# The last column half of two output products, run token tile by token tile

## Chip, core and metric

The kernel runs on one core of a Trainium2 chip. The metric is the device time of one execution in microseconds: 1674.59 us, the median of three runs of the kernel before (1671.56 to 1675.25).

## What is computed

One inference step of a 2-layer encoder, for a prompt of 256 tokens and 8 samples of 16 tokens (128 rows); width 1024, all in fp32. Shortened:

```
for l in range(2):
    x = x + mixer(rms_norm(x)) @ w_out[l]          # attention, retention and convolution heads, joined
    q = rms_norm(x) @ wx_q[l]                      # cross attention, 4 heads, 256 memory tokens
    x = x + softmax(q @ k_mem) @ v_mem @ wx_o[l]
    h = rms_norm(x)
    x = x + (dense_swiglu(h) if l == 0 else moe_swiglu(h))   # top 2 of 8 experts in layer 1
y = rms_norm(x)
```

The change lies at two places in each layer: the product with `w_out` and what follows it (norm, product with `wx_q`), and the product with `wx_o` and what follows it (norm, dense network or router).

## The kernel before

**Tiles and slabs.** The 384 tokens are three tiles of 128 (`NT` = 3). A weight of 1024 x 1024 comes in four slabs of 128 x 2048 (1 MB): a left and a right column half of 512, and of each two row halves. SyncE fetches the slabs in one fixed order into a ring of four slots (`R`). For slab s it waits for the reader of slab s-4, which the function `slabs` names: for `w_out` the tile of the product whose end frees the slot, for the query and output weights of cross attention the low part (below) that was made of the slab.

**Split products.** An fp32 slab is split in a high part (a copy by ScalarE, `w_high` L926, in the dense network L803) and a low part (a subtraction by VectorE, `w_low` L930, `mix_low` L967, L808). A product of a tile with half a slab's depth is then three matmuls per 128 rows (L1151 to L1153): one column half of one token tile is 8 x 3 = 24 matmuls of 512 columns. The last halves of `out` (`mix_product`) and of `o` (`split_product`) run slab by slab: tiles 0, 1, 2 with the first slab, then tiles 0, 1, 2 with the second.

**Between products.** Per token tile: VectorE adds the product to the residual `x` (`add_x`, L2196, one instruction per column half), ScalarE squares it with a row sum (`squares`, L1724), GpSimd makes the reciprocal root (L2552, L2554), VectorE scales the row (`norm_row`, L2150), TensorE transposes it in eight pieces (`norm`, L1077), ScalarE takes the high part (`h_high`, L1731) and VectorE the low part (`take`, L2162) into `hT_parts`. All of it is in a program order of its own on each engine, written out by hand; nothing is reordered when it runs. `psum_jobs` lists which PSUM bank each product takes and in which order.

**Names at the two places.** `part(l, m, low)` tells where the split query and output slabs m = 0 to 7 lie (0 to 3 the query weight, 4 to 7 the output weight; m = 6, 7 are the right half of the output weight). Before, some of them shared space with others, so `w_high` waited for the end of a product. SyncE waits at L1007 for the last tile of `o` in layer 0, and only then streams the dense network's slabs (L836). `prime` frees the dense network's slots and signals for their first use.

## Time and profile before

| | us |
|---|---|
| median of 3 runs | 1674.59 |
| profiled execution, device time | 1668.94 |
| its span, first to last instruction | 1667.0 |
| TensorE busy in it | 1542.4 (93%) |
| VectorE busy | 1003.5 (60%) |
| ScalarE busy | 747.3 (45%) |
| GpSimd busy | 184.3 (11%) |

The mean granted clock of TensorE is 0.97 of full speed. The share of busy time is a mean over stages with different limits; what a seam between two products is worth is read from the timelines of that seam.

### The profile page before, as it was taken

Reading aid. Unit: us, or ns where it says so; the run is one execution under the profiler, and the core shown is the slowest. Engines: PE = TensorE matmul, PEld = TensorE weight load, DVE = VectorE, ACT = ScalarE, POOL = GpSimd, SP = SyncE. Lnnn points to the kernel's source line nnn. Section 1 sums busy time; section 2 is a strip of 40 time slices with the busy share of each in tenths; the row PEclk is TensorE's granted clock in tenths of the full one; section 3 lists DMA queues with packets and bytes.
Section 4 is the critical chain, followed back from the end, with each engine's and each line's share of the span. In section 5 each row is a group of like instructions: output and inputs, shape, how many; then the busy total and the mean of one; then the engine's idle time right before and its main releaser. Section 6 shows DMA issues by size and latency. Waiting matters only on the chain.

```text
span 1667.0 us, 21420 instructions
## 1 busy us (share of the span) xinstructions
PE 1542.4 (93%) x7995; PEld 1262.3 (76%) x7995; DVE 1003.5 (60%) x1304; ACT 747.3 (45%) x896; POOL 184.3 (11%) x270
## 2 busy tenths in 40 slices
PE   5999999797999999899999997979999999999996
PEld 4875677666998898688567775768887888788875
DVE  3692653444342434359365434367988898888986
ACT  3423333433332333242243343146676667666763
POOL 2351200000000000314220000100000000000001
PEclk9999999998999999899999999869999999999998
DMA  6735354374333333343645329269999999999993
GB/s 225 250 109 189 130 164 152 146 271 156 111 119 120 130 100 110 127 144 125 195 152 173 134 76 353 102 234 332 316 323 320 332 329 329 325 335 335 317 329 124
DMA packets 176576, 347.72 MB, mean 209 GB/s; under 512 B 7114, under 2 KB 48348, under 8 KB 176240
## 3 DMA queue, kind: packets, MB, share of 16 engines
q1 hardware_dynamic: 162224, 316.17, 55.4%
q0 software_dynamic: 5936, 19.92, 3.5%
q10 hardware_dynamic: 8352, 10.75, 1.8%
q8 instruction: 44, 0.72, 0.2%
q14 instruction: 20, 0.16, 0.0%
HBM read 335.20 MB, written 13.48 MB: 209 GB/s over the span
## 4 chain that ended last, share of the span: by engine, by line
PE 59%; issue 22%; DMA 8%; DVE 6%; ACT 3%; POOL 2%; POOLq 0%; SPq 0%; DVEq 0%; ACTq 0%
PE bank L1151 14%; PE bank L1153 14%; PE bank L1152 14%; PE bank L1113 5%; DMA arena<-h_rows,row_of_slot 4%; PE bank L1077 4%; PE bank L1528 2%; DMA ring<-in_cache_mem_k 1%; POOL counts L2609 1%; DMA out_new_mem_k_prompt<-arena 1%; DVE arena L2325 1%; ACT arena L1719 1%; PE bank L1580 1%; PE bank L1649 1%; DVE arena_parts L808 1%
## 5 line engine op out<-in xcount | busy, mean ns | idle before, releaser
L808 DVE TENSOR_TENSOR arena_parts<-ring,arena_parts 128x2048 fp32r<-128x2048 f32 (+1 forms) x156 | 331.3, 2142 | 176.9 <-ACT arena_parts L803 176.9
L1151 PE MATMUL bank<-arena_parts,features_parts 128*128 128x512 f32 (+2 forms) x1056 | 410.5, 389 | 13.1 <-DVE ring_low_parts L967 7.3
L1153 PE MATMUL bank<-arena_parts 128*128 128x512 f32 (+1 forms) x928 | 363.1, 391 | 0.0
L803 ACT ACTIVATE arena_parts<-ring 128x2048 fp32r<-128x2048 f32 (+1 forms) x156 | 277.4, 1796 | 148.3 <-PE bank L1153 132.9
L1152 PE MATMUL bank<-arena_parts 128*128 128x512 f32 (+1 forms) x704 | 258.9, 368 | 0.0
L1152 PE MATMUL bank<-arena_parts,features_parts 128*128 128x512 f32 (+1 forms) x672 | 257.4, 383 | 0.0
L1151 PEld LDWEIGHTS bank<-arena_parts,features_parts 128*128 128x128 f32 x1056 | 201.3, 191 | 51.9 <-issue 11.1
L1153 PEld LDWEIGHTS bank<-arena_parts 128*128 128x128 f32 x928 | 176.2, 190 | 40.1
L1719 ACT ACTIVATE arena<-bank 128x512 f32<-128x512 f32 (+3 forms) x160 | 85.3, 568 | 228.9 <-PE bank L1153 138.4
L1153 PE MATMUL bank<-arena_parts,features_parts 128*128 128x512 f32 (+1 forms) x480 | 182.0, 379 | 0.0
L1152 PE MATMUL bank<-ring_low_parts,features_parts 128*128 128x512 f32 (+1 forms) x384 | 146.6, 382 | 0.0
L1151 PE MATMUL bank<-arena_parts 128*128 128x512 f32 x352 | 141.9, 403 | 5.0 <-DVE arena_parts L808 5.0
L1152 PEld LDWEIGHTS bank<-arena_parts,features_parts 128*128 128x128 f32 x672 | 127.4, 190 | 23.1
L1152 PEld LDWEIGHTS bank<-arena_parts 128*128 128x128 f32 x704 | 133.3, 189 | 14.5
L1151 PE MATMUL bank<-features_parts,arena_parts 128*128 128x384 f32 x352 | 119.4, 339 | 9.5 <-DVE arena_parts L808 9.5
L1077 PE MATMUL bank<-consts,arena 128*128 128x128 f32 (+1 forms) x576 | 81.7, 291 | 48.5 <-DVE arena L2150 17.1
L808 DVE TENSOR_TENSOR arena_parts<-mem_kv,arena_parts 128x2048 fp32r<-128x2048 f32 (+1 forms) x60 | 120.1, 2017 | 5.2 <-ACT arena_parts L803 5.2
L1153 PE MATMUL bank<-features_parts,arena_parts 128*128 128x384 f32 x352 | 119.5, 339 | 0.0
L1077 PEld LDWEIGHTS bank<-consts,arena 128*128 128x128 f32 (+1 forms) x576 | 69.5, 149 | 65.8 <-issue 38.0
L803 ACT ACTIVATE arena_parts<-mem_kv 128x2048 fp32r<-128x2048 f32 (+1 forms) x60 | 102.0, 1700 | 31.2 <-PE bank L1153 31.2
L1153 PEld LDWEIGHTS bank<-arena_parts,features_parts 128*128 128x128 f32 x480 | 90.6, 189 | 14.7
L967 DVE TENSOR_TENSOR ring_low_parts<-ring,arena_parts 128x2048 fp32r<-128x2048 f32 (+1 forms) x32 | 69.5, 2172 | 45.1 <-ACT arena_parts L962 44.8
(288 smaller groups left out, 1913.0 us busy)
## 6 DMA issues: line engine op xcount, KB each, us to landing
ring<-in_moe_w_up SPq DMA_DIRECT2D x40, 1024.0 KB, 6.2
ring<-in_moe_w_down SPq DMA_DIRECT2D x30, 1024.0 KB, 5.2
ring<-in_w_in SPq DMA_DIRECT2D x20, 1024.0 KB, 7.4
ring<-in_moe_w_gate SPq DMA_DIRECT2D x20, 1024.0 KB, 7.4
mem_kv<-in_moe_w_gate SPq DMA_DIRECT2D x20, 1024.0 KB, 9.1
ring<-in_cache_mem_k SPq DMA_DIRECT2D x16, 1024.0 KB, 7.4
ring<-in_cache_mem_v SPq DMA_DIRECT2D x16, 1024.0 KB, 8.0
ring<-in_moe_w_gate SPq DMA_DIRECT2D x20, 768.0 KB, 5.7
```

The source lines that it names most:

```text
L803: nc.scalar.activation(self.part(s, 0), self.raw(s), ACT.Copy).then_inc(self.high, 1)
L808: nc.vector.tensor_tensor(self.part(s, 1), self.raw(s), self.part(s, 0).bitcast(F32), ALU.subtract).then_inc(self.split["v"], 1)
L967: nc.vector.tensor_tensor(low, raw, high.bitcast(F32), ALU.subtract).then_inc(s_msplit, 1)
L1077: return nc.tensor.transpose(out, src, ident[0:src.shape[0], 0:src.shape[0]])
L1113: ins = nc.tensor.matmul(out[:, 0:w], left(k, t), wt[:, k - k0, :], start=(g == 0 and k == k0), stop=(g == len(groups) - 1 and k == k0 + n ...
L1151: nc.tensor.matmul(out, left[0], right[0], start=start, stop=False)
L1152: nc.tensor.matmul(out, left[0], right[1], start=False, stop=False)
L1153: return nc.tensor.matmul(out, left[1], right[0], start=False, stop=stop)
L1528: ins = nc.tensor.matmul(b[:, :], memT[:, k, t * P:(t + 1) * P], wt[:, k - 4 * g, :], start=(k == 0), stop=(k == KC - 1))
L1580: ins = nc.tensor.matmul(b[:, i * 256:(i + 1) * 256], qxT[:, 2 * h + k, (j // 2) * P:(j // 2 + 1) * P], mkT[:, 2 * h + k, :], start=(k == ...
L1649: ins = nc.tensor.matmul(b[:, i * 256:(i + 1) * 256], mv[:, mt, (2 * h + i) * P:(2 * h + i + 1) * P], pxT[:, h, mt, :], start=(mt == 0), s ...
L1719: st.emptied(A(out, in_, ACT.Copy), *key)
```

## The change

It makes five moves.

- The right halves of `out` and `o` run tile by tile (`last_chunk`): each tile with both slabs, then the next. Tile 0's transposes stand ahead of tile 2's matmuls. With it, the slot of the third slab of `w_out` is freed by the last tile instead of the first (`slabs`).
- The transposes of tiles 1 and 2 ahead of `q` move: tile 1's stand before the first tile of `q`, tile 2's behind it.
- VectorE takes tile 0 and scales tile 1 between the residual adds; at the seam to `q` the low part of the query slab m = 2 now stands ahead of the scaled row of tile 2.
- The slabs m = 6 and 7 get space of their own, so their parts are made before `o`'s right half, and their low parts stand around its first residual add.
- SyncE's wait before the dense slabs is gone; in layer 0 the slots are freed right behind m = 7's low part.

```diff
@@ psum_jobs
+    def tiles_last(name, n):
+        product(name, 1, NT, "v")
+        for t in range(NT):
+            if t == NT - 1:
+                norm(n, (0,))
+            jobs.append((name + (1, t), (3 * (big[0] % 2) + t,), "v"))
+        big[0] += 1
...
@@ slabs
-                last = tiles - 1 if half or (c == 0 and key[0] == "in") else 0
+                last = tiles - 1 if half or (c == 0 and key[0] == "in") or (c == 1 and key[0] == "out") else 0
...
@@ part, w_high
-        OWN_AT = {(4, 0): 2 * NT * D, (4, 1): n_.at, (5, 0): 0, (5, 1): n_.at + SLAB, (7, 0): 2 * NT * D, (7, 1): n_.at}
+        OWN_AT = {(4, 0): 2 * NT * D, (4, 1): n_.at, (5, 0): 0, (5, 1): n_.at + SLAB,
+                  (6, 0): n_.at - 3 * SLAB, (6, 1): n_.at - 2 * SLAB, (7, 0): n_.at - SLAB, (7, 1): n_.at + 2 * SLAB}
...
-            if m >= NSPLIT and m not in (4, 5):
-                q = m - NSPLIT
-                key = ("q", l, 0, NT - 1) if q < 2 else ("q", l, 1, NT - 1 if q == 3 else 0) if q < 4 else ("o", l, 0, NT - 1)
-                wait_filled(act, *key)
+            if m == NSPLIT:
+                wait_filled(act, "q", l, 0, NT - 1)
+            elif m >= 6:
+                wait_filled(act, "xss", l, 3)
...
@@ SyncE
                 if s == at_layer:
-                    wait_filled(sp, "o", 0, 1, NT - 1)
                     with sp.Fori(0, half_ffn.n) as i:
...
@@ TensorE
+            def last_chunk(key, n, left, slabs_):
+                wt = []
+                for t in range(NT):
+                    if t == NT - 1:
+                        norm(n, (0,))
+                    b = begin(*key, 1, t)
+                    for g in range(2):
+                        if t == 0:
+                            wt.append(slabs_[g]())
+                        ins = split_tile(b, left, 4 * g, wt[g], t)
+                    end(ins, *key, 1, t)
...
-                for c in range(2):
-                    mix_product(("out", l), l, MIX + 2 * c, hT_parts, 512, c,
-                                {2: ("obT", l, 1), 4: ("obT", l, 3)} if c == 0 else {})
-
-                norm(3 * l + 1, (0,))
+                mix_product(("out", l), l, MIX, hT_parts, 512, 0, {2: ("obT", l, 1), 4: ("obT", l, 3)})
+                last_chunk(("out", l), 3 * l + 1, hT_parts, [lambda: mix_slab(l, MIX + 2), lambda: mix_slab(l, MIX + 3)])
+
+                norm(3 * l + 1, (1,))
                 wt = [w_parts(l, m) for m in range(2)]
                 for t in range(NT):
+                    if t == 1:
+                        norm(3 * l + 1, (2,))
                     wait_emptied(pe, "hT", 3 * l + 1, t, 1)
                     b = begin("q", l, 0, t)
                     for g in range(2):
-                        if g and t < NT - 1:
-                            norm(3 * l + 1, (t + 1,))
                         ins = split_tile(b, hT_parts, 4 * g, wt[g], t)
...
-                split_product(("o", l), l, 6, oT_parts, 1)
-
+                last_chunk(("o", l), 3 * l + 2, oT_parts, [lambda: w_parts(l, 6), lambda: w_parts(l, 7)])
+
+                wait_emptied(pe, "hT", 3 * l + 2, 0, 1)
                 (routed if l % 2 else half_ffn).prime(turn(bank[7][:, 0:P], ident))
-                norm(3 * l + 2)
+                norm(3 * l + 2, (1, 2))
...
@@ ScalarE, at both seams
-                squares(3 * l + 1, (0, 1))
+                squares(3 * l + 1, (0,))
                 h_high(3 * l + 1, (0,))
-                squares(3 * l + 1, (2,))
+                squares(3 * l + 1, (1, 2))
...
@@ VectorE, norm_T
+                if n % 3:
+                    take(1)
+                    if n % 3 == 1:
+                        w_low(dve, n // 3, 2)
+                    norm_row(n, 2)
+                    take(2)
+                    if n % 3 == 1:
+                        w_low(dve, n // 3, 3)
+                    return
...
@@ VectorE, add_x
                         if (c, t) == (1, 0):
                             norm_row(n, 0)
+                        if (c, t) == (1, 1):
+                            take_T(n, 0)
+                            norm_row(n, 1)
...
-                        if name == "o" and (c, t) in ((0, 0), (0, NT - 1)):
-                            w_low(dve, l, 6 + (t > 0))
+                        if name == "o" and (c, t) == (0, 0):
+                            w_low(dve, l, 7)
+                            if l == 0:
+                                half_ffn.prime(V.memset(full[:, 2:3], 0.0), "split")
...
@@ VectorE, before add_x of "o"
                 values_low(3)
+                w_low(dve, l, 6)
                 add_x("o", l, 3 * l + 2)
```

VectorE from the two low parts of the query slabs m = 0, 1 (L930) to those of m = 2 and 3, before (L2196 is the residual add, L2150 the scaled row, L2162 the low part of a transposed tile):

```order
L930 TENSOR_TENSOR arena_parts<-ring,arena_parts 128x2048 [waits cross_slab_high_part_ready] x2
L2196 TENSOR_TENSOR x<-bank,x 128x512 [waits psum_filled]
L2150 SCALAR_TENSOR_TENSOR arena<-x,stat,arena 128x1024 [waits rstd_ready,gain_row_in1]
L2196 TENSOR_TENSOR x<-bank,x 128x512 [waits psum_filled] x2
L2162 TENSOR_TENSOR arena_parts<-bank,features_parts 128x4x128 [waits h_high_part_ready,psum_filled] x2
L2150 SCALAR_TENSOR_TENSOR arena<-x,stat,arena 128x1024 [waits rstd_ready] x2
L2162 TENSOR_TENSOR arena_parts<-bank,features_parts 128x4x128 [waits h_high_part_ready,psum_filled] x2
L930 TENSOR_TENSOR arena_parts<-ring,arena_parts 128x2048 [waits cross_slab_high_part_ready]
L2162 TENSOR_TENSOR arena_parts<-bank,features_parts 128x4x128 [waits h_high_part_ready,psum_filled] x2
L930 TENSOR_TENSOR arena_parts<-ring,arena_parts 128x2048 [waits cross_slab_high_part_ready]
```

The same stretch of VectorE after (L940, L2225, L2172 and L2183 are the same four):

```order
L940 TENSOR_TENSOR arena_parts<-ring,arena_parts 128x2048 [waits cross_slab_high_part_ready] x2
L2225 TENSOR_TENSOR x<-bank,x 128x512 [waits psum_filled]
L2172 SCALAR_TENSOR_TENSOR arena<-x,stat,arena 128x1024 [waits rstd_ready,gain_row_in1]
L2225 TENSOR_TENSOR x<-bank,x 128x512 [waits psum_filled]
L2183 TENSOR_TENSOR arena_parts<-bank,features_parts 128x4x128 [waits h_high_part_ready,psum_filled] x2
L2172 SCALAR_TENSOR_TENSOR arena<-x,stat,arena 128x1024 [waits rstd_ready]
L2225 TENSOR_TENSOR x<-bank,x 128x512 [waits psum_filled]
L2183 TENSOR_TENSOR arena_parts<-bank,features_parts 128x4x128 [waits h_high_part_ready,psum_filled] x2
L940 TENSOR_TENSOR arena_parts<-ring,arena_parts 128x2048 [waits cross_slab_high_part_ready]
L2172 SCALAR_TENSOR_TENSOR arena<-x,stat,arena 128x1024 [waits rstd_ready]
L2183 TENSOR_TENSOR arena_parts<-bank,features_parts 128x4x128 [waits h_high_part_ready,psum_filled] x2
L940 TENSOR_TENSOR arena_parts<-ring,arena_parts 128x2048 [waits cross_slab_high_part_ready]
```

The transposed tile 0 and the scaled row of tile 1 now stand between the residual adds, and the low part of m = 2 stands ahead of the scaled row of tile 2, not behind it.

TensorE at the end of `out`, before (L1077 is a transpose of tile 0, the matmuls behind it are the first of `q`):

```order
L1152 MATMUL bank<-arena_parts,features_parts 128x512
L1153 MATMUL bank<-arena_parts 128x512
L1077 MATMUL bank<-consts,arena 128x128 [waits psum_emptied_by_vector,h_ready]
L1077 MATMUL bank<-consts,arena 128x128 x3
L1077 MATMUL bank<-consts,arena 128x128 [waits psum_emptied_by_vector]
L1077 MATMUL bank<-consts,arena 128x128 x3
L1151 MATMUL bank<-arena_parts,features_parts 128x512
L1152 MATMUL bank<-arena_parts,features_parts 128x512
L1153 MATMUL bank<-arena_parts 128x512
```

TensorE after, at the end of tile 1 of `out`'s right half (L1086 the transposes of tile 0, L1160 to L1162 behind them tile 2 of `out`):

```order
L1160 MATMUL bank<-arena_parts,features_parts 128x512
L1161 MATMUL bank<-ring_low_parts,features_parts 128x512
L1162 MATMUL bank<-arena_parts 128x512
L1086 MATMUL bank<-consts,arena 128x128 [waits psum_emptied_by_vector,h_ready]
L1086 MATMUL bank<-consts,arena 128x128 x3
L1086 MATMUL bank<-consts,arena 128x128 [waits psum_emptied_by_vector]
L1086 MATMUL bank<-consts,arena 128x128 x3
L1160 MATMUL bank<-arena_parts,features_parts 128x512 [waits psum_emptied_by_vector]
L1161 MATMUL bank<-ring_low_parts,features_parts 128x512
```

The transposes of tile 0 have 24 matmuls of `out` behind them, and the wait for the scaled row (`h_ready`) stands inside the product.

## Rows read from the trace of the kernel before

**Rows 1.** The page: the span, and the chain that ended last, by engine.

```profile
span 1667.0 us, 21420 instructions
...
PE 59%; issue 22%; DMA 8%; DVE 6%; ACT 3%; POOL 2%; POOLq 0%; SPq 0%; DVEq 0%; ACTq 0%
```

**Rows 2.** TensorE timeline, `out` to `q` (last row layer 1): start, us, instruction, idle.

```profile
252.64 0.39 PE L1152 MATMUL bank<-ring_low_parts,features_parts 128*128 128x512 f32 x1
...
254.24 0.39 PE L1153 MATMUL bank<-arena_parts 128*128 128x512 f32 x1
254.47 1.03 PE L1077 MATMUL bank<-consts,arena 128*128 128x128 f32 x8
257.35 0.47 PE L1151 MATMUL bank<-arena_parts,features_parts 128*128 128x512 f32 x1 [1.85 <-DVE arena_parts L2162]
...
932.36 0.47 PE L1151 MATMUL bank<-arena_parts,features_parts 128*128 128x512 f32 x1 [1.85 <-DVE arena_parts L2162]
```

**Rows 3.** Timeline of TensorE, `o` to the dense product, layer 0.

```profile
392.83 1.04 PE L1077 MATMUL bank<-consts,arena 128*128 128x128 f32 x8
...
399.39 1.94 PE L1077 MATMUL bank<-consts,arena 128*128 128x128 f32 x8 [0.92 <-DVE arena_parts L2162]
407.74 0.68 PE L1151 MATMUL bank<-features_parts,arena_parts 128*128 128x384 f32 x1 [6.41 <-DVE arena_parts L808]
```

**Rows 4.** Timeline of VectorE, the same stretch.

```profile
405.31 4.49 DVE L808 TENSOR_TENSOR arena_parts<-ring,arena_parts 128x2048 fp32r<-128x2048 f32 x2 [2.54 <-ACT arena_parts L803]
```

**Rows 5.** Timeline of ScalarE, same stretch.

```profile
393.46 1.09 ACT L1731 ACTIVATE features_parts<-bank 128x512 fp32r<-128x512 f32 x2 [0.16 <-PE bank L1077]
394.44 1.06 ACT L1724 ACTIVATE arena<-x 128x1024 f32<-128x1024 f32 x1
...
402.07 1.28 ACT L803 ACT_TABLE_LOAD   x1
403.37 5.51 ACT L803 ACTIVATE arena_parts<-ring 128x2048 fp32r<-128x2048 f32 x3
```

**Rows 6.** Waits of SyncE's queue, 350 to 420 us: total, times, longest.

```profile
SPq L1007 <- PE bank L1153: 36.8, 1, 36.8
```

**Rows 7.** DMA issues: size, median us to landing: q2; third dense slab.

```profile
ring<-in_wx_q SPq DMA_DIRECT2D x1, 1024.0 KB, 4.9
...
ring<-in_ffn_w_up SPq DMA_DIRECT2D x1, 1024.0 KB, 10.7
```

**Rows 8.** Timeline of VectorE, `out` to `q`, layer 0.

```profile
245.17 2.29 DVE L930 TENSOR_TENSOR arena_parts<-ring,arena_parts 128x2048 fp32r<-128x2048 f32 x1 [1.86 <-ACT arena_parts L926]
249.17 0.69 DVE L2196 TENSOR_TENSOR x<-bank,x 128x512 f32<-128x512 f32 x1 [1.71 <-PE bank L1153]
252.10 1.29 DVE L2150 SCALAR_TENSOR_TENSOR arena<-x,stat,arena 128x1024 f32<-128x1024 f32 x1 [2.24 <-POOL stat L2554]
...
263.78 2.29 DVE L930 TENSOR_TENSOR arena_parts<-ring,arena_parts 128x2048 fp32r<-128x2048 f32 x1 [0.94 <-ACT arena_parts L926]
```

**Rows 9.** Timeline of TensorE, `o` to the router, layer 1.

```profile
1075.58 1.94 PE L1077 MATMUL bank<-consts,arena 128*128 128x128 f32 x8 [0.72 <-DVE features_T L2164]
```

**Rows 10.** Timeline of SyncE: the issue of slab q2, layer 0.

```profile
249.16 0.37 SPq L1038 DMA_DIRECT2D ring<-in_wx_q  x1
```

**Rows 11.** Timeline of ScalarE, layer 0: high part of q2.

```profile
261.83 1.92 ACT L926 ACTIVATE arena_parts<-ring 128x2048 fp32r<-128x2048 f32 x1
```

**Rows 12.** Windows: busy time and count by engine, granted clock, DMA.

```profile
core 0: us, PE busy (x) PEld busy (x) DVE busy (x) ACT busy (x) POOL busy (x), PEclk, DMA share, GB/s
...
257.35:261.00 3.65, 3.65 (x20) 3.06 (x21) 2.22 (x2) 0.14 (x1) 1.52 (x2) 1.00 1.06 419
...
932.36:937.00 4.64, 4.64 (x15) 3.64 (x16) 2.21 (x2) 0.00 (x0) 1.52 (x2) 0.63 1.04 416
...
397.00:407.70 10.70, 3.41 (x16) 2.64 (x14) 6.33 (x8) 8.10 (x9) 0.93 (x2) 0.50 0.77 292
```

**Rows 13.** Timeline of TensorE in the key stage, layer 0.

```profile
334.71 1.54 PE L1077 MATMUL bank<-consts,ring 128*128 128x128 f32 x6 [5.30 <-DMA ring<-in_cache_mem_k]
```

More of the change, by code:

```diff
@@ L228, in psum_jobs @@
             wide(("obT", l, b), "v")
-        product(("out", l), 2, NT, "v")
-        norm(3 * l + 1, range(NT - 1))
+        tiles_last(("out", l), 3 * l + 1)
+        norm(3 * l + 1, (1,))
         first_chunk(("q", l), 3 * l + 1)
@@ L261, in psum_jobs @@
         wide(("xvT", l, 3), "v")
-        product(("o", l), 2, NT, "v")
-        norm(3 * l + 2)
+        tiles_last(("o", l), 3 * l + 2)
+        norm(3 * l + 2, (1, 2))
         if l % 2:
@@ L1545, in _ @@
                 wait_emptied(pe, "ocT", l, 1)
-                for c in range(2):
-                    mix_product(("out", l), l, MIX + 2 * c, hT_parts, 512, c,
-                                {2: ("obT", l, 1), 4: ("obT", l, 3)} if c == 0 else {})
-                norm(3 * l + 1, (0,))
+                mix_product(("out", l), l, MIX, hT_parts, 512, 0, {2: ("obT", l, 1), 4: ("obT", l, 3)})
+                last_chunk(("out", l), 3 * l + 1, hT_parts, [lambda: mix_slab(l, MIX + 2), lambda: mix_slab(l, MIX + 3)])
+                norm(3 * l + 1, (1,))
                 wt = [w_parts(l, m) for m in range(2)]
                 for t in range(NT):
+                    if t == 1:
+                        norm(3 * l + 1, (2,))
                     wait_emptied(pe, "hT", 3 * l + 1, t, 1)
@@ L1677, in _ @@
                     end(split_tile(bank[BANK[("o", l, 0, t)][0]], oT_parts, 4, wo[1], t), "o", l, 0, t)
-                split_product(("o", l), l, 6, oT_parts, 1)
+                last_chunk(("o", l), 3 * l + 2, oT_parts, [lambda: w_parts(l, 6), lambda: w_parts(l, 7)])
+                wait_emptied(pe, "hT", 3 * l + 2, 0, 1)
                 (routed if l % 2 else half_ffn).prime(turn(bank[7][:, 0:P], ident))
-                norm(3 * l + 2)
+                norm(3 * l + 2, (1, 2))
                 wait_emptied(pe, "hT", 3 * l + 2, NT - 1, 1)
@@ L2013, in _ @@
                 w_high(act, l, 7)
-                squares(3 * l + 2, (0, 1))
+                squares(3 * l + 2, (0,))
                 if l % 2 == 0:
                     h_high(3 * l + 2, (0,))
-                squares(3 * l + 2, (2,))
+                squares(3 * l + 2, (1, 2))
                 act.wait_ge(s_st, 16 * 8 * (l + 1))
@@ L2151, in norm_row, with take_T, norm_T @@
                                               ALU.mult, ALU.mult), s_h)
-            def norm_T(n, rows_left=NT):
-                def take(t):
-                    for half in range(2):
-                        wait_filled(dve, "hT", n, t, half)
-                        at_ = (slice(None), slice(4 * half, 4 * half + 4), slice(t * P, (t + 1) * P))
-                        b = bank[BANK[("hT", n, t, half)][0]][:, :].rearrange("p (k n) -> p k n", k=4)
-                        if n < 5:
-                            dve.wait_ge(s_hpart, 2 * NT * n + 2 * t + half + 1)
-                            ins = V.tensor_tensor(hT_parts[1][at_], b, hT_parts[0][at_].bitcast(F32), ALU.subtract)
-                        else:
-                            ins = V.tensor_copy(hT[at_], b)
-                        st.emptied(ins, "hT", n, t, half)
+            def take_T(n, t):
+                for half in range(2):
+                    wait_filled(dve, "hT", n, t, half)
+                    at_ = (slice(None), slice(4 * half, 4 * half + 4), slice(t * P, (t + 1) * P))
+                    b = bank[BANK[("hT", n, t, half)][0]][:, :].rearrange("p (k n) -> p k n", k=4)
+                    if n < 5:
+                        dve.wait_ge(s_hpart, 2 * NT * n + 2 * t + half + 1)
+                        ins = V.tensor_tensor(hT_parts[1][at_], b, hT_parts[0][at_].bitcast(F32), ALU.subtract)
+                    else:
+                        ins = V.tensor_copy(hT[at_], b)
+                    st.emptied(ins, "hT", n, t, half)
+            def norm_T(n):
+                def take(t):
+                    take_T(n, t)
+                if n % 3:
[7 more added lines that the diff above has]
+                    return
                 if n == 3:
                     mix_low(dve, 1, 0)
-                if rows_left == NT:
-                    norm_row(n, 0)
+                norm_row(n, 0)
                 if n == 3:
@@ L2180, in norm_T @@
                 take(1)
-                if n in (1, 4):
-                    w_low(dve, n // 3, 2)
                 take(2)
-                if n in (1, 4):
-                    w_low(dve, n // 3, 3)
-                if n in (0, 3):
-                    mix_low(dve, n // 3, 2)
+                mix_low(dve, n // 3, 2)
             def add_x(name, l, n):
@@ L2457, in _ @@
                 add_x("out", l, 3 * l + 1)
-                norm_T(3 * l + 1, NT - 1)
+                norm_T(3 * l + 1)
                 wait_filled(dve, "q", l, 1, NT - 1)
@@ L2529, in _ @@
                 values_low(3)
+                w_low(dve, l, 6)
                 add_x("o", l, 3 * l + 2)
-                (routed if l % 2 else half_ffn).prime(V.memset(full[:, 2:3], 0.0), "split")
-                norm_T(3 * l + 2, NT - 1)
+                if l % 2:
+                    routed.prime(V.memset(full[:, 2:3], 0.0), "split")
+                norm_T(3 * l + 2)
                 if l % 2:
```

## Prediction

> **What bounds the kernel now.** I read the page first: TensorE leads the chain that ended last, with 59%, in a span of 1667.0 us [rows 1]. Where TensorE runs without a gap only fewer matmuls would help, and the change keeps them all. So the question is where TensorE waits. I therefore read the four seams that the change touches, in TensorE's timeline, and then the engines that end its waits. (q0 to q3 are the four half slabs of the query weight, o6 and o7 the last two of the output weight; a "turn" is a transpose by TensorE, eight per token tile and 1.03 us for the eight.)
>
> At the seam from `out` to `q`, matmuls follow each other every (254.24 - 252.64) / 7 = 0.229 us, then comes tile 0's turn, and then a wait of 1.85 us that VectorE ends; it is 1.85 in layer 1 too [rows 2]. That is all there is to gain at this seam: 1.85 us a layer, plus what the clock loses after it. At the seam behind `o` in layer 0, TensorE is free at 392.83 and the dense product begins at 407.74, its last wait 6.41 us long and ended by VectorE's low part of a weight slab [rows 3]. VectorE in turn had waited 2.54 us for ScalarE [rows 4], which did the turned rows' high parts, then a table load of 1.28 us at 402.07, and the first slab's high part at 403.37 [rows 5].
>
> **The early dense stream.** SyncE waited 36.8 us for the end of `o` before it issued the first dense slab [rows 6], and now issues it once the low part of o7 is done, behind the first residual add of `o`: some 20 us earlier (three tiles of 5.5 us and the rest of the left half). I price this at nothing. ScalarE reaches the first slab only after all turned rows and the table load, and before that load it isn't waiting for a transfer [rows 5]; the order of its work there stays, but for one Square that goes behind tile 0's high part. Even the third slab of the burst took only 10.7 us [rows 7], so it had landed some 2 us after ScalarE took the first, and before its turn. What a faster first slab could give would be the idle time of ScalarE, which is not there. The transfers now run beside `o`, where TensorE reads weights that have already landed, so I see no price either.
>
> **The `o` seams.** With tiles run one by one, tile 0's turn (1.03) sits ahead of tile 2's matmuls and needs nothing new: its row is ready long before. Tile 2 then ends at 392.83 + 1.03 = 393.86 instead of 392.83, since the turn itself has only changed places. From there the chain to tile 2's own turn is: about 0.1 to start the residual add, 0.69 for it (as in [rows 8]), 1.06 for ScalarE's Square and some 0.2 to read its sum, 1.09 for tile 1's high part, which now comes behind that Square [rows 5], 0.6 for the last piece of tile 1's low part, and 1.29 for the normed row. That is 393.86 + 4.95 = 398.8, against 399.39 [rows 3]. So -0.6 us; the rest of the seam follows unchanged. In layer 1 the same turn begins at 1075.58 [rows 9] and I take -0.6 again, although no high part stands in that chain. Together **-1.2**, between 0 (the row later by half a microsecond) and -3 (turns at full clock).
>
> **The `q` seams.** Here the change moves three things, and each runs into a queue. I work them out for layer 0.
> - Left half of `out` filled: slab q2 went out at 249.16, when tile 0's right half was done [rows 10], 48 matmuls after the left half, so that was at 249.16 - 48 x 0.229 = 238.2. The tiles of the right half are now filled at 238.2 + 24 x 0.229 = 243.7 and at 249.2.
> - VectorE's residual add of tile 0 stands behind the low part of q1, which ends at 245.17 + 2.29 = 247.46 [rows 8]. Before, that cost nothing, since the tile came at 249.17. From that add to the normed row went 252.10 + 1.29 - 249.17 = 4.22 us [rows 8]. So the row is there at 247.46 + 4.22 = 251.7, while TensorE is free for its turn at about 249.0: **a new wait of 2.7 us**. Turn and tile 2 then run to 251.7 + 1.03 + 5.5 = 258.2.
> - Slab q2's ring slot was released by the first tile of `out`'s right half; since all three tiles now read both halves, the reader is the last tile. It is issued at about 258.4 instead of 249.16, lands 4.9 us later [rows 7], at 263.3, and takes 1.92 on ScalarE [rows 11] and 2.29 on VectorE [rows 8]: 267.5. On VectorE the normed row of tile 2 is queued behind that low part. It ends at 267.5 + 1.29 = 268.8. TensorE meanwhile does tile 1's turn and the first tile of `q`: 258.2 + 1.03 + 5.5 = 264.8. Next on TensorE is tile 2's turn: **a new wait of 4.0 to 4.1 us**. The wait of 1.85 is gone.
>
> So 2.7 + 4.1 - 1.85 = +5.0 a layer. Layer 1 has the same rows 675.0 us later, so **+10.0**. Bounds: 4 to 6 a layer, that is 8 to 12, by a landing that is up to half a microsecond either way and the pieces between instructions.
>
> **The clock.** After the same wait of 1.85 the window of layer 0 shows a granted clock of 1.00, that of layer 1 0.63 [rows 12]: the lower level, 1.2 GHz, for a part of it, which cost 4.64 x (1 - 0.63) = 1.7 us. After the gaps behind `o` the clock was 0.50 [rows 12]. There will be four new waits, all longer than 1.85. The two of 4.1 I count as followed by such a stretch, of the two of 2.7 one: 3 x 1.7 - 1.7 = **+3.4**, between -1.7 (none) and +5.1 (all four). The Trainium skill, page "TensorE: Matmul & The Clock Gate", section "What's actually happening", says that the throttled state is the default and that activity releases it. By that alone every one of the four would pay, and this term would be +5.1, the sum 13.9; layer 0's window at 1.00 after a wait shows that not every wait does.
>
> **Sum.** 10.0 + 3.4 - 1.2 = 12.2 us. The profiled execution took 1668.94 us (a span of 1667.0 and 1.94 around it), 5.65 below the median of 1674.59, so its 12.2 would give 1681.1 there; I add them to the median, and round: **1687**. From the bounds, 8 - 1.7 - 3 = +3 and 12 + 5.1 + 0 = +17: 1678 to 1692.
>
> **Rivals.** (1) Faster: the seams close as they are laid out. If q2 were split by the time tile 0 of `q` ends, and q1's low part did not hold the add, TensorE would have neither wait: 2 x -1.85 - 1.7 - 1.2 = -6.6, so 1668. The point is q2's landing: its two splits and the row take 1.92 + 2.29 + 1.29 = 5.5, so it must have landed by 264.8 - 5.5 = 259.3, 0.9 us after its issue. For it speaks that everything else on that path is short; against it, the 4.9 [rows 7]. It holds also if the slot is released earlier than I read. 0.09.
> (2) No change: the delay is absorbed by a later wait that doesn't move. In the key stage TensorE waits 5.30 us for a transfer [rows 13]; two such would take the 10 us back, and leave 1674.6 + 3.4 - 1.2 = 1677 or less. Against it: the slot of that transfer is released by TensorE's own reads, so it moves along. 0.08.
> (3) Slower still: q2, q3 and the first two key slabs are now issued in one burst and share the bandwidth. If q2 lands like the third of a burst, 10.7 instead of 4.9 [rows 7], TensorE waits 5.8 longer in each layer: 1687 + 11.6 = 1698.6. Against it: in the one burst there is, the later slabs took the longer time. The Trainium skill, page "DMA: Bandwidth & Descriptors", section "Queues, rings and completion order", says that each DMA engine consumes descriptors in ring order, which by itself would put q2 first; no run here has shown that for this burst. 0.05.
>
> **How the numbers follow.** The forecast gets 0.78. A difference below 0.2% (3.3 us) can't be told from none; the forecast's low end just touches that, for 0.01. Faster 0.09 from rival 1; same 0.08 + 0.01 = 0.09; slower 0.77 + 0.05 = 0.82. The range goes from 1675 (half of rival 2 with it) to 1692, and leaves out rival 1, rival 3 and half of rival 2, some 0.18.
>
> **What would show it.** In the trace after: a wait of TensorE of about 2.7 us before the turn ahead of tile 2 of `out`, ended by a normed row, and one of about 4 us one tile into `q`, ended by the normed row of tile 2, which starts as the low part of q2 ends; ScalarE waiting for the transfer of q2, issued at the end of `out`; a granted clock well below 1 in `q`. Behind `o`, dense slabs issued at some 373 instead of 393.8 and the dense product beginning only 0.6 us earlier relative to the end of `o`. I am wrong if q2 is issued inside `out`, if the normed row of tile 2 precedes q2's low part, or if the dense product starts several microseconds sooner.

## The result: 1683.71 us after, 1671.56 before

Five runs each: 1683.71 us (1681.42 to 1687.70) against 1671.56 (1668.81 to 1675.25). The ratio is 1.0073, with a 95% interval of 1.005 to 1.0097: 12.15 us slower, between 8 and 16. The forecast was +12.2; the time that went with it, 1687, lies 3.3 us higher since it started from 1674.59, the median of three runs. One of out_only's six runs (below) fell into a slower state (2231.77 us at a mean granted clock of 0.65), so its time is the median of the other five. Of the two executions with a profile, that of before (1668.94) lies as low as the lowest of these five (1668.81) and that of after is the longest of its own (1687.70), so their 18.8 us are not the difference of the kernels; a second profile of before, below, shows what of it is chance.

### The seam from `out` to `q`, after

TensorE's timeline of after, layer 0 and then layer 1 (start, duration, instruction, idle time before it and what ended it). It answers to [rows 2], where one wait of 1.85 us stood in each layer:

```profile
254.39 1.97 PE L1086 MATMUL bank<-consts,arena 128*128 128x128 f32 x8 [2.53 <-DVE arena L2172]
...
262.43 1.03 PE L1086 MATMUL bank<-consts,arena 128*128 128x128 f32 x8
...
273.10 1.97 PE L1086 MATMUL bank<-consts,arena 128*128 128x128 f32 x8 [4.04 <-DVE arena L2172]
...
941.35 1.09 PE L1086 MATMUL bank<-consts,arena 128*128 128x128 f32 x8 [2.50 <-DVE arena L2172]
...
958.52 1.97 PE L1086 MATMUL bank<-consts,arena 128*128 128x128 f32 x8 [4.10 <-DVE arena L2172]
```

At 254.39 stands the turn of tile 0, ahead of tile 2 of `out`; at 262.43 tile 1's, with no wait; at 273.10 tile 2's, one tile into `q`. Waits of 2.53 and 4.04 us, and 2.50 and 4.10 in layer 1: all four are ended by VectorE's scaled row (L2172).

VectorE's timeline of the same stretch, layer 0 (L940 is a low part, L2225 the residual add, L2172 the scaled row), which answers to [rows 8]:

```profile
247.91 2.29 DVE L940 TENSOR_TENSOR arena_parts<-ring,arena_parts 128x2048 fp32r<-128x2048 f32 x1 [1.88 <-ACT arena_parts L936]
250.12 0.68 DVE L2225 TENSOR_TENSOR x<-bank,x 128x512 f32<-128x512 f32 x1
253.05 1.28 DVE L2172 SCALAR_TENSOR_TENSOR arena<-x,stat,arena 128x1024 f32<-128x1024 f32 x1 [2.24 <-POOL stat L2590]
...
269.56 2.29 DVE L940 TENSOR_TENSOR arena_parts<-ring,arena_parts 128x2048 fp32r<-128x2048 f32 x1 [3.17 <-ACT arena_parts L936]
271.77 1.28 DVE L2172 SCALAR_TENSOR_TENSOR arena<-x,stat,arena 128x1024 f32<-128x1024 f32 x1
```

The add of tile 0's right half begins at 250.12, as the low part of q1 ends, with no idle time before it; the row follows, 250.12 to 254.33 = 4.2 us. At 271.77 the scaled row of tile 2 begins as the low part of q2 ends. Why that was late shows in the timelines of SyncE and ScalarE and in the DMA issues (size, us to landing), which answer to [rows 10], [rows 11] and [rows 7]:

```profile
262.63 0.37 SPq L1047 DMA_DIRECT2D ring<-in_wx_q  x1
```

```profile
267.61 1.91 ACT L936 ACTIVATE arena_parts<-ring 128x2048 fp32r<-128x2048 f32 x1 [2.13 <-DMA ring<-in_wx_q]
```

```profile
ring<-in_wx_q SPq DMA_DIRECT2D x1, 1024.0 KB, 5.0
```

q2 is issued at 262.63, when the last tile of `out` is done, lands 5.0 us later, and ScalarE, idle for 2.13 us until then, makes the high part to 269.52.

Windows behind the four waits of after (busy time and count by engine, granted clock, DMA share, GB/s), and behind the two waits of before, which answer to [rows 12]:

```profile
core 0: us, PE busy (x) PEld busy (x) DVE busy (x) ACT busy (x) POOL busy (x), PEclk, DMA share, GB/s
254.39:262.40 8.01, 8.01 (x32) 6.80 (x33) 3.21 (x4) 2.23 (x4) 0.75 (x2) 0.79 0.01 2
...
273.10:285.00 11.90, 11.90 (x45) 9.86 (x46) 1.38 (x2) 2.38 (x4) 0.00 (x0) 0.78 0.37 146
941.35:949.30 7.95, 7.95 (x43) 6.80 (x44) 3.81 (x5) 2.71 (x5) 0.75 (x2) 1.00 0.06 4
...
958.52:970.00 11.48, 11.48 (x42) 9.52 (x43) 1.38 (x2) 2.37 (x4) 0.00 (x0) 0.75 0.39 152
```

```profile
257.35:269.00 11.65, 11.65 (x59) 9.64 (x60) 6.77 (x7) 4.58 (x6) 1.52 (x2) 1.00 0.78 288
...
932.36:944.00 11.64, 11.64 (x51) 9.50 (x52) 5.79 (x5) 3.62 (x5) 1.52 (x2) 0.85 0.66 247
```

What such a window, full of matmuls, loses to the clock is its length times one less the granted clock. After: 8.01 x 0.21 = 1.7, 11.9 x 0.22 = 2.6, nothing, and 11.48 x 0.25 = 2.9, together 7.2 us. Before: nothing, and 11.64 x 0.15 = 1.75.

### The seam behind `o`, after

TensorE in layer 0, which answers to [rows 3]; the turn of tile 1, the turn of tile 2, the first matmul of the dense product:

```profile
406.84 1.04 PE L1086 MATMUL bank<-consts,arena 128*128 128x128 f32 x8
411.93 1.97 PE L1086 MATMUL bank<-consts,arena 128*128 128x128 f32 x8 [4.05 <-DVE arena L2172]
420.30 0.68 PE L1160 MATMUL bank<-features_parts,arena_parts 128*128 128x384 f32 x1 [6.41 <-DVE arena_parts L817]
```

ScalarE in the same stretch ([rows 5]) and the issue of the dense slabs by SyncE:

```profile
413.94 0.60 ACT L1753 ACTIVATE features_parts<-bank 128x512 fp32r<-128x512 f32 x1 [0.26 <-PE bank L1086]
...
414.64 1.28 ACT L812 ACT_TABLE_LOAD   x1
415.94 5.51 ACT L812 ACTIVATE arena_parts<-ring 128x2048 fp32r<-128x2048 f32 x3
```

```profile
385.76 1.03 SPq L845 DMA_DIRECT2D ring<-in_ffn_w_gate  x2
```

From the first of these turns to the dense product it was 407.74 - 392.83 = 14.91 us before and is 420.30 - 406.84 = 13.46 now, of which 1.03 are the turn of tile 0 that was only moved ahead. The dense slabs are issued at 385.76, 21 us ahead of the end of `o` instead of 1 us behind it, and the last wait is 6.41 us as before: ScalarE comes from its last high part almost straight (one small instruction between) to the table load and the first slab.

### The profile page after: what moved, and what is told of

Same layout as the page of the kernel before. It is cut to its first block, busy times and chain, and to the rows that moved or that the text cites. A ratio compares the mean times of both kernels' runs of the same rounds, so it can differ in the third digit from the quotient of the medians.

```text
span 1685.8 us, 21422 instructions
## 1 busy us (share of the span) xinstructions
PE 1547.6 (92%) x7995; PEld 1266.7 (75%) x7995; DVE 1004.0 (60%) x1304; ACT 747.4 (44%) x896; POOL 183.4 (11%) x270
## 4 chain that ended last, share of the span: by engine, by line
PE 57%; issue 22%; DMA 10%; DVE 6%; ACT 3%; POOL 2%; POOLq 0%; SPq 0%; DVEq 0%; ACTq 0%
PE bank L1160 13%; PE bank L1161 13%; PE bank L1162 13%; PE bank L1122 5%; DMA arena<-h_rows,row_of_slot 4%; PE bank L1086 4%; DMA ring<-in_cache_mem_k 2%; PE bank L1550 2%; DMA ring<-in_wx_q 1%; POOL counts L2645 1%; DMA ring<-in_cache_mem_v 1%; DMA out_new_mem_k_prompt<-arena 1%; DVE arena L2359 1%; PE bank L1601 1%; PE bank L1670 1%
## 5 line engine op out<-in xcount | busy, mean ns | idle before, releaser
L1160 PE MATMUL bank<-arena_parts,features_parts 128*128 128x512 f32 (+2 forms) x1056 | 411.8, 390 | 12.1 <-DVE ring_low_parts L977 10.0
L1162 PE MATMUL bank<-arena_parts 128*128 128x512 f32 (+1 forms) x928 | 363.3, 391 | 0.0
L1160 PEld LDWEIGHTS bank<-arena_parts,features_parts 128*128 128x128 f32 x1056 | 202.1, 191 | 50.5 <-issue 7.0
L1162 PEld LDWEIGHTS bank<-arena_parts 128*128 128x128 f32 x928 | 176.9, 191 | 40.2
L1162 PE MATMUL bank<-arena_parts,features_parts 128*128 128x512 f32 (+1 forms) x480 | 181.6, 378 | 0.0
L1160 PE MATMUL bank<-arena_parts 128*128 128x512 f32 x352 | 141.9, 403 | 5.0 <-DVE arena_parts L817 5.0
L1086 PE MATMUL bank<-consts,arena 128*128 128x128 f32 (+1 forms) x576 | 81.3, 290 | 61.9 <-DVE arena L2172 32.2
L1160 PE MATMUL bank<-features_parts,arena_parts 128*128 128x384 f32 x352 | 120.9, 343 | 9.5 <-DVE arena_parts L817 9.5
L1086 PEld LDWEIGHTS bank<-consts,arena 128*128 128x128 f32 (+1 forms) x576 | 68.7, 148 | 79.5 <-issue 37.2
L1162 PE MATMUL bank<-features_parts,arena_parts 128*128 128x384 f32 x352 | 120.1, 341 | 0.0
L1162 PEld LDWEIGHTS bank<-arena_parts,features_parts 128*128 128x128 f32 x480 | 90.5, 189 | 14.9
```

The costliest lines, as they stand in the source:

```text
L1086: return nc.tensor.transpose(out, src, ident[0:src.shape[0], 0:src.shape[0]])
L1160: nc.tensor.matmul(out, left[0], right[0], start=start, stop=False)
L1162: return nc.tensor.matmul(out, left[1], right[0], start=False, stop=stop)
```

## Two executions of the kernel before

**before_again.** The kernel before, unchanged.

> The kernel before, unchanged, for a second profile of it: how far do two executions differ stage by stage? Its first profiled execution (1668.94) lies low among its 23 timed runs (median 1672.8). Theory (the stretches at the lower clock differ from execution to execution, behind the same waits): the waits of the seams repeat within 0.1 us, and the stages that differ by over 1 us are those with another granted clock, the start of the dense product among them. Rival: the waits themselves differ.

It took 1673.98 us. The table gives the time between landmarks in TensorE's timeline, each the first instruction behind a wait that every trace shows; an entry is the difference of two starts.

| stretch | before | before_again | after | row0_first |
|---|---|---|---|---|
| start to the sample's keys | 158.98 | 160.66 | 160.46 | 159.28 |
| to the cross attention, through `out` and `q` | 138.80 | 138.80 | 148.96 | 136.74 |
| to the sample's memory keys | 36.93 | 36.98 | 36.95 | 36.99 |
| to the dense product, through `o` | 73.03 | 73.22 | 73.93 | 74.61 |
| to its second pass | 142.35 | 145.32 | 144.36 | 142.60 |
| to layer 1 | 144.66 | 144.66 | 145.80 | 144.67 |
| to the sample's keys, layer 1 | 137.74 | 137.40 | 136.85 | 136.22 |
| through `out` and `q`, layer 1 | 141.84 | 141.87 | 147.83 | 138.19 |
| to the memory keys | 37.02 | 36.90 | 37.07 | 36.88 |
| through `o` to the expert numbers | 81.99 | 82.30 | 80.42 | 81.47 |
| to the end | 573.66 | 573.89 | 573.17 | 573.45 |

Between the two executions of one kernel the start differs by 1.7 us, the first dense pass by 3.0, all else by at most 0.35. The waits at the four seams repeat, as the theory said (1.85 and 6.41 us in both). One far ahead of them doesn't: in the products ahead of `out` TensorE waits 2.41 us in one and 4.60 in the other for VectorE's low parts, and goes on at 116.00 and at 117.14; that is 1.1 of the start's 1.7. So of the 18.8 us between the profiles 1.5 (start) and 2.0 (first dense pass) are of the kind that one kernel shows by itself; the 1.1 of the second pass these two executions don't show (144.66 in both), the last section does. The change is in the rows through `out` and `q`: +10.2 and +6.0.

Of the +10.2, 1.2 us lie at the start of that stretch, where the kernel is the same, from the sample's keys to the next wait that all traces show (windows of after, then before; the granted clock is third from the end):

```profile
160.46:169.44 8.98, 7.80 (x76) 5.14 (x76) 6.71 (x14) 4.00 (x8) 0.00 (x0) 0.81 0.38 119
...
158.98:166.72 7.74, 6.30 (x77) 4.24 (x77) 6.68 (x14) 3.89 (x8) 0.00 (x0) 1.00 0.43 135
```

This piece takes 7.74 us in nine of the fourteen traces and 8.94 to 8.98 in five, both_moved and row0_first_o_before among them, so it goes with neither the waits at `q` nor the order at `o`. What is left, 8.9 + 6.0 = 14.9 us, is what the four waits and the windows behind them add up to: 2.53 + 4.04 + 2.50 + 4.10 - 2 x 1.85 = 9.5 of waits and 7.2 - 1.75 = 5.4 of clock.

## One part alone

**out_only**: only `out` and its seam to `q` are new. (This cut and the others show the lines that matter of an edit; against the changed kernel where nothing else is said.)

```diff
-        tiles_last(("o", l), 3 * l + 2)
-        norm(3 * l + 2, (1, 2))
+        product(("o", l), 2, NT, "v")
+        norm(3 * l + 2)
...
-                last_chunk(("o", l), 3 * l + 2, oT_parts, [lambda: w_parts(l, 6), lambda: w_parts(l, 7)])
+                split_product(("o", l), l, 6, oT_parts, 1)
```

> The changed kernel with everything at `o` and behind it as before: only `out` and its seam to `q` are new. Theory (the loss lies in VectorE's queue at the seam to `q`, twice): the kernel before plus 2 x 5.0 of waits and about 3.4 of clock, 1671.6 + 13.4 = 1685, with TensorE's waits of 2.5 and 4.0 us in both layers as in the changed kernel. Rival (the early dense stream and the new order at `o` share in the loss): half of it, about 1678 to 1679.

1687.87 us against 1672.81, ratio 1.0089 (1.0072 to 1.0106): +15, between 12 and 18; in the stretches through `out` and `q` +9.95 and +5.8 (with the 1.2 at the start, as in after). The loss lies there whole.

**o_only**: only `o`, its slabs' space and the early dense stream are new.

```diff
-        tiles_last(("out", l), 3 * l + 1)
-        norm(3 * l + 1, (1,))
+        product(("out", l), 2, NT, "v")
+        norm(3 * l + 1, range(NT - 1))
...
-                last = tiles - 1 if half or (c == 0 and key[0] == "in") or (c == 1 and key[0] == "out") else 0
+                last = tiles - 1 if half or (c == 0 and key[0] == "in") else 0
```

> The changed kernel with `out` and its seam to `q` as before: only `o`, the space of the slabs 6 and 7, and the early dense stream are new. Theory: -1.2 us, 1670.4, between 1668 and 1672; the dense product begins some 0.5 us sooner against the end of `o`, the first dense slab is issued 20 us sooner. Rival (early transfers collide, or the dense product starts at the lower clock for longer, as it did in the trace after by 2 us): +2 to +4, 1674 to 1676.

1667.35 us, ratio 0.997 (0.9956 to 0.9985): -5.5, between -2.5 and -7.4, more than the forecast's -1.2.

**o_only_sp_wait**: the early stream undone in it (the line against o_only).

```diff
                 if s == at_layer:
+                    wait_filled(sp, "o", 0, 1, NT - 1)
```

> o_only with SyncE's wait for the end of `o` put back ahead of the dense slabs: the early dense stream alone is undone. o_only was 5.5 us below the kernel before, where -1.2 had been forecast. Theory (the early stream brings nothing, ScalarE reaches the first slab no sooner): the same as o_only, 1667 to 1668. Rival (the early stream is the part that gains): back to -1.5, about 1671.

1668.47 us, ratio 0.9977 (0.996 to 0.9993). The 1.1 us between the two medians can't be told from nothing, and the interval, 1666.3 to 1671.8, just holds the rival's 1671 as well. What speaks for the theory is the trace: the wait ahead of the dense product is 6.41 us here, in o_only and in the kernel before alike, wherever the slabs are issued.

**o_only_again** repeats o_only.

> o_only once more, for what the part at `o` is worth: by the seams in the traces, 1.0 to 2.5 us less than the kernel before, 1669 to 1670.5; by the medians of o_only and o_only_sp_wait 4.5 to 5.5 less, 1666 to 1667. In its trace the cadence of the matmuls in the dense product, at a granted clock of 1.00, is either 0.173 or 0.177 us, as in the two executions of the kernel before (0.1733 and 0.1767); if the new order sets the faster one, it is 0.173 again.

1669.58 us, ratio 0.9983 (0.9967 to 1.0), the cadence (last section) 0.1756: neither of the two. So the new order doesn't set it.

## The two waits, one by one

**row2_first**: on VectorE the scaled row of tile 2 stands ahead of the low part of q2.

```diff
                     take(1)
-                    if n % 3 == 1:
-                        w_low(dve, n // 3, 2)
                     norm_row(n, 2)
+                    if n % 3 == 1:
+                        w_low(dve, n // 3, 2)
                     take(2)
```

> The changed kernel with one edit on VectorE: at the seam to `q` the scaled row of tile 2 stands ahead of the low part of q2. Theory: the wait of 4.0 us ahead of tile 2's turn goes in both layers, the clock loss behind it too: 1683.7 - 8.1 - 3.4 = 1672. Rival (the late landing of q2 is the bound itself, or tile by tile order costs TensorE time by itself): TensorE waits for q2 a few microseconds later instead, 1682 to 1684.

1670.56 us, ratio 0.9987 (0.9972 to 1.0002): 13 us less than after, for one swap; the two waits (4.04 + 4.10) and the clock behind them (2.6 + 2.9) come to 13.6. TensorE's turns of tiles 0 and 2, layer 0, and VectorE's scaled row of tile 2 and low part of q2:

```profile
253.00 1.09 PE L1086 MATMUL bank<-consts,arena 128*128 128x128 f32 x8 [2.39 <-DVE arena L2172]
...
265.90 1.03 PE L1086 MATMUL bank<-consts,arena 128*128 128x128 f32 x8
```

```profile
263.29 1.27 DVE L2172 SCALAR_TENSOR_TENSOR arena<-x,stat,arena 128x1024 f32<-128x1024 f32 x1
266.61 2.29 DVE L940 TENSOR_TENSOR arena_parts<-ring,arena_parts 128x2048 fp32r<-128x2048 f32 x1 [2.04 <-ACT arena_parts L936]
```

The wait of 4 us is gone, that of 2.4 stays. q2 is split as late as before (266.61 to 268.90), and nobody waits for it: its late landing held TensorE only through the row that stood behind it.

**q1_behind_add**: the other wait alone.

```diff
                             w_low(dve, l, 0)
-                            w_low(dve, l, 1)
...
                         if (c, t) == (1, 0):
+                            if name == "out":
+                                w_low(dve, l, 1)
                             norm_row(n, 0)
```

> The changed kernel with the low part of q1 behind the residual add of tile 0's right half; the scaled row of tile 2 stays behind the low part of q2. Theory: the wait ahead of tile 0's turn falls from 2.5 to 0.7 us in both layers, the one of 4.0 us behind it stays at about 4 and keeps its clock loss: both_moved plus 2 x 4.0 and 2 to 6 us of clock, 1674 to 1678. Rival (the two waits are not independent: tile 2 ends sooner, so q2 is issued sooner and the second wait shrinks as well): 1668 to 1670.

1678.13 us, ratio 1.0039 (1.0022 to 1.0055). The turns of tiles 0 and 2 in layer 0:

```profile
252.26 0.98 PE L1086 MATMUL bank<-consts,arena 128*128 128x128 f32 x7 [0.50 <-DVE arena L2172]
...
269.44 1.43 PE L1086 MATMUL bank<-consts,arena 128*128 128x128 f32 x8 [4.10 <-DVE arena L2172]
```

The first wait falls to 0.50 and the second stays at 4.10 (0.57 and 4.21 in layer 1): the two are independent.

**both_moved**: both edits.

> As row2_first, and the low part of q1 stands behind the residual add of tile 0's right half instead of ahead of it. Theory: the wait of 2.5 us ahead of tile 0's turn goes too, in both layers, with its clock loss: no wait over 0.5 us is left at the seam to `q`, where the kernel before has 1.85 twice and 1.7 of clock in one layer: 1671.6 - 3.7 - 1.7 - 1.2 = 1665. Rival (something next in line, such as the low part of q1 for the second half of tile 0 of `q`, or the key stage's transfers, takes it back): 1671 to 1673.

1663.5 us, ratio 0.9953 (0.9938 to 0.9968): 9 us faster than the kernel before, where 1665 was expected. 0.74 us of wait are left ahead of tile 0's turn in layer 0.

**row0_first**: both_moved, with the low part of q1 behind the scaled row of tile 0 too (the cut against both_moved).

```diff
                         if (c, t) == (1, 0):
-                            if name == "out":
-                                w_low(dve, l, 1)
                             norm_row(n, 0)
+                            if name == "out":
+                                w_low(dve, l, 1)
```

> both_moved with one more swap on VectorE: the scaled row of tile 0 stands ahead of the low part of q1, not behind it. Theory: the last wait at the seam, 0.74 us ahead of tile 0's turn, goes in both layers: 1663.5 - 1.5 = 1662. Rival (the low part of q1 is then late for the first tile of `q`, or the residual add of tile 1 behind it): 1664 to 1667.

1662.5 us, ratio 0.9941 (0.9918 to 0.9965). The turns of tiles 0 and 2 in layer 0, and ScalarE's high part of q2:

```profile
249.27 1.04 PE L1086 MATMUL bank<-consts,arena 128*128 128x128 f32 x8
...
262.13 1.03 PE L1086 MATMUL bank<-consts,arena 128*128 128x128 f32 x8
```

```profile
260.85 1.91 ACT L936 ACTIVATE arena_parts<-ring 128x2048 fp32r<-128x2048 f32 x1 [2.15 <-DMA ring<-in_wx_q]
```

No turn waits, and q2's high part begins at 260.85, with its wait for the transfer still there, off TensorE's path. This is the lowest time of those tried, some 21 us below the changed kernel, though its 1 us below both_moved is within the spread of either.

**row0_first_o_before**: the same with `o` as before.

> row0_first with `o` and everything behind it as before: what the part at `o` is worth on another base. By the seams in the traces (1.9 us less from the end of `o` to the next product, over both layers): 1662.5 + 1.9 = 1664.4. By the medians of o_only and o_only_sp_wait: 1662.5 + 5 = 1667.5.

1666.56 us, ratio 0.9971 (0.9956 to 0.9986): the part at `o` is worth 4 us here, between the two expectations and not able to tell them apart, since row0_first's own interval is some 4 us either way.

## The clock apart from the waits

**filled_waits**: the changed kernel with its waits, but TensorE turns the identity matrix while it waits.

```diff
                     if t == NT - 1:
+                        if key[0] == "out":
+                            b = begin(*key, 1, t)
+                            for _ in range(17):
+                                turn(b[:, 0:P], ident)
                         norm(n, (0,))
...
                     if t == 1:
+                        b = begin("q", l, 0, t)
+                        for _ in range(29):
+                            turn(b[:, 0:P], ident)
                         norm(3 * l + 1, (2,))
```

> The changed kernel, all its waits kept, but TensorE turns the identity matrix into the bank of its next product while it waits: 17 times ahead of tile 0's turn at `out`, 29 times one tile into `q` (some 2.2 and 3.7 us), in both layers. What it computes is the same. Theory (the waits cost 9.5 us, and another 7.2 at the lower clock behind three of the four in the trace after): the two long waits end at the same time as before, the clock behind them stays at 1.00, 1683.7 - 5 to 7 = 1677 to 1679. Rival (the clock behind a wait doesn't hang on what TensorE does in it, or the fillers come too late): 1683 or more.

1676.47 us, ratio 1.0032 (1.0018 to 1.0045): 7.2 less than after. TensorE in layer 0, and two windows of the same stretch:

```profile
250.74 2.02 PE L1086 MATMUL bank<-consts 128*128 128x128 f32 x17
253.45 1.09 PE L1086 MATMUL bank<-consts,arena 128*128 128x128 f32 x8 [0.69 <-DVE arena L2179]
...
266.35 3.33 PE L1086 MATMUL bank<-consts 128*128 128x128 f32 x29
270.89 1.09 PE L1086 MATMUL bank<-consts,arena 128*128 128x128 f32 x8 [1.22 <-DVE arena L2179]
```

```profile
251.00:262.00 11.00, 10.31 (x63) 8.80 (x61) 5.15 (x6) 3.38 (x8) 1.50 (x4) 1.00 0.08 8
...
271.00:283.00 12.00, 12.00 (x56) 9.83 (x57) 1.29 (x2) 2.15 (x4) 0.00 (x0) 1.00 0.34 134
```

From free to the turn it is 250.74 to 253.45 = 2.7 and 266.35 to 270.89 = 4.5 us, no shorter than the waits of after (in layer 1 2.6 and 4.2), and the clock is 1.00 behind all four. So the waits keep their price, and what went is the clock's: 7.2 us by the medians, each known to 2 to 4 us, and 7.2 by the windows above.

**row0_first_filled**: row0_first, with the same filling behind `o` in layer 0 (the cut against row0_first).

```diff
-                norm(3 * l + 2, (1, 2))
+                spare = bank[BANK[("o", l, 0, 0)][0]]
+                norm(3 * l + 2, (1,))
+                if l == 0:
+                    for _ in range(29):
+                        turn(spare[:, 0:P], ident)
+                norm(3 * l + 2, (2,))
+                if l == 0:
+                    for _ in range(45):
+                        turn(spare[:, 0:P], ident)
```

> row0_first with the same filling behind `o` in layer 0: 29 turns of the identity between the turns of tiles 1 and 2, 45 behind tile 2's. Theory: the turn of tile 2 runs at full clock (about 0.9 us sooner to the dense product), and the dense product starts at full clock (0.79 to 0.90 over its first 14 us so far, 1.4 to 2.9 us): 1662.5 - 3 = 1659.5. Rival (the fillers reach beyond the waits or the low clock has another cause): 1662 to 1664.

1662.85 us, ratio 0.9947 (0.993 to 0.9964): no gain that can be measured against row0_first. TensorE, and the window of the dense product's start:

```profile
395.24 3.33 PE L1086 MATMUL bank<-consts 128*128 128x128 f32 x29
399.46 1.09 PE L1086 MATMUL bank<-consts,arena 128*128 128x128 f32 x8 [0.88 <-DVE arena L2180]
400.38 5.08 PE L1086 MATMUL bank<-consts 128*128 128x128 f32 x45
407.01 0.44 PE L1160 MATMUL bank<-features_parts,arena_parts 128*128 128x384 f32 x1 [1.55 <-DVE arena_parts L817]
```

```profile
411.00:425.00 14.00, 14.00 (x81) 14.00 (x81) 2.56 (x2) 5.42 (x7) 0.00 (x0) 1.00 0.68 236
```

The clock does stay at 1.00, into the dense product. But that pass took 142.78 us, row0_first's, with a start at the lower clock, 142.60. In this execution the matmuls themselves came slower (last section: 529 of them, 0.0034 us each, 1.8 us), which took back what the start had won; whether several profiles would show the gain is open.

## Why the prediction was right

- **The waits** (+10.0 forecast): +9.5. Each came where it was put, behind the instruction that was named, and row2_first and q1_behind_add remove them one by one.
- **The clock** (+3.4): the count was right, three stretches of four; the size was not. They cost 1.7, 2.6 and 2.9 us rather than 1.7 each, so the term is +5.4, just beyond its upper bound of 5.1. The step that failed was to price a stretch behind a wait of 4 us by one behind a wait of 1.85. What the Trainium skill says in "TensorE: Matmul & The Clock Gate", section "What's actually happening" (throttled by default, released by activity), agrees with filled_waits, where filling the waits with turns kept the granted clock at 1.00. What the prediction drew from it, that every wait would pay, doesn't hold: the wait of 2.50 us in layer 1 is followed by a window at 1.00.
- **The `o` seams** (-1.2, between 0 and -3): the terms listed for the chain to tile 2's turn add up to 5.03 us, not the 4.95 that was used, so by its own terms the forecast was -0.5 a layer rather than -0.6. In after the chain took 411.93 - 406.84 = 5.09. In nine traces with the new order, those without fillers there, the time from the end of `o` to the dense product is 12.8 to 13.6 us in layer 0, where the four with the old order have 15.0 to 15.1; in layer 1, to the expert numbers, it is 21.4 to 22.2 against 23.8. Less the moved turn that is -0.4 to -1.2 and -0.6 to -1.3, some -1.7 in all. The medians say -5.5, -4.5 and -2.9, each with some 2.5 us either way, and by differences of two kernels, less sharp, -4.1 (row0_first) and -2.9 (after less out_only). So the term was too small, by some 0.5 us as the traces have it; the 1 to 4 us by which the medians give more are in no stretch that the traces single out, and whether they are the order's or chance stays open.
- **The early stream** (nothing): borne out by the wait of 6.41 us, which is the same with and without it; the times of o_only and o_only_sp_wait are too close to tell.
- **The sum** came out at 12.15 for 12.2, and that it did to the tenth is luck: the seams to `q` cost 9.5 + 5.4 = 14.9 by the trace (out_only: +15), not 13.4, and `o` gave more than 1.2. By the traces the sum is 14.9 - 1.7 = 13.2, by the medians of `o` between 9 and 12; the measured interval, 8 to 16, holds them all.
- **Rival 1** asked that q2 land within 0.9 us of its issue; it took 5.0. For the order as written that was the right condition, but it left out the cheaper way: in row0_first q2 lands as slowly (5.0 us) and TensorE waits nowhere at this seam, since tile 2's row no longer stands behind q2's low part. The rival's price for seams to `q` without a wait, 2 x -1.85 - 1.7 = -5.4, agrees with row0_first_o_before (1666.56 - 1671.27 = -4.7, between -2.3 and -7.4). **Rival 2** didn't happen: the stretch behind `q`, with the long wait for a transfer, takes 36.95 and 37.07 us in the two layers, as it did (36.93 and 37.02). **Rival 3** didn't either: q2, first in its burst, took 5.0 us. That agrees with the Trainium skill, page "DMA: Bandwidth & Descriptors", section "Queues, rings and completion order", which says that each DMA engine consumes descriptors in ring order.
- Not tried: to issue q2 inside `out`, by freeing the slot sooner. With all tiles reading both halves that would be a race.

## To carry to other kernels

When a loop's order is changed, look at what then stands ahead of the small steps in the in-order queues of the other engines: here two swaps of VectorE instructions turned 12 us of loss into 9 us of gain, with TensorE's order untouched. The late transfer of q2 cost nothing once nothing urgent was queued behind its consumer. And price a wait of TensorE with the lower clock that may follow it: at these seams that was half as much again.

## What the runs showed of the hardware

**One kernel, several cadences.** TensorE in the dense product, matmuls of 384 columns, before and before_again (11 steps from the first row to the last):

```profile
440.01 0.34 PE L1152 MATMUL bank<-arena_parts 128*128 128x384 f32 x1
...
441.92 0.34 PE L1151 MATMUL bank<-features_parts,arena_parts 128*128 128x384 f32 x1
```

```profile
444.96 0.34 PE L1153 MATMUL bank<-features_parts,arena_parts 128*128 128x384 f32 x1
...
446.90 0.34 PE L1152 MATMUL bank<-arena_parts 128*128 128x384 f32 x1
```

The step is 1.91 / 11 = 0.174 and 1.94 / 11 = 0.176 us, and 0.1733 and 0.1767 over 40 us of matmuls at a granted clock of 1.00: 2% apart. The first dense pass has 529 such matmuls, so that is 529 x 0.0034 = 1.8 of the 3.0 us between these two executions. Most of the rest is the clock at its start (windows of before and before_again, the granted clock third from the end):

```profile
407.74:421.74 14.00, 14.00 (x73) 14.00 (x74) 6.38 (x3) 4.83 (x4) 0.00 (x0) 0.90 0.65 226
...
409.66:423.66 14.00, 14.00 (x65) 14.00 (x66) 5.03 (x3) 3.83 (x3) 0.00 (x0) 0.80 0.65 225
```

14 x 0.10 = 1.4 us. All fourteen traces have one of three cadences in this pass, 0.1733 (six), 0.1755 to 0.1756 (three, after among them) or 0.1767 (five), the same all through the pass once the clock is at 1.00. It belongs to the pass and not to the execution: before_again had 0.1767 in the first pass and 0.1733 in the second. In after the second pass has 0.1755 against 0.1733 in before, 528 x 0.0022 = 1.2 us, which is the 1.1 in the table. No row here says why.

**A transfer whose landing time varies.** The four sample value slabs of layer 0 landed in 7.7 us (median of the four) in o_only and 9.6 in o_only_again, issued alike; the other traces lie between:

```profile
ring<-in_cache_mem_v SPq DMA_DIRECT2D x4, 1024.0 KB, 7.7
```

```profile
ring<-in_cache_mem_v SPq DMA_DIRECT2D x4, 1024.0 KB, 9.6
```

With the longer ones TensorE waits, in the changed kernel too (1.84 us at 366.31, which is why its stretch through `o` in the table is longer than before although the seam is shorter). Here the wait in o_only_again:

```profile
356.26 3.06 PE L1644 MATMUL bank<-ring,arena 128*32 128x512 f32 x16 [2.00 <-DMA ring<-in_cache_mem_v]
```
